# Strassen's algorithm for 18 of the 22 up-projection pairs of the second FFN

## The reference

```
x = x + 0.5 * rmsnorm(swiglu(rmsnorm(x, g0), w1, w3, w2), g1)      # first FFN
x = x + rmsnorm(mixer(rmsnorm(x, g2)), g3)                          # mLSTM, S5, short convolution
x = x + 0.5 * rmsnorm(swiglu(rmsnorm(x, g4), w1', w3', w2'), g5)    # second FFN
swiglu(x, w1, w3, w2) = (silu(x @ w1) * (x @ w3)) @ w2
```

## Time and profile before

| | us |
|---|---|
| median of 3 runs | 1088.48 (1088.02 to 1089.86) |
| span of the profiled execution | 1087.4 |
| TensorE busy | 1077.2 (99%) |
| VectorE busy | 533.9 (49%) |
| ScalarE busy | 358.4 (33%) |
| GpSimd busy | 95.5 (9%) |
| chain that ended last: TensorE's share | 95% |

### The profile page before, as it was taken

One profiled execution on the slowest core, in us unless ns is written; L12 is line 12 of the kernel. 1 busy time (PEld: TensorE's weight loads), 2 busy tenths in 40 slices (PEclk: granted clock), 3 DMA queues, 4 the chain that ended last, 5 costly groups with the idle time before them and its releaser, 6 DMA issues.

```text
span 1087.4 us, 21585 instructions
## 1 busy us (share of the span) xinstructions
PE 1077.2 (99%) x8945; PEld 1063.8 (98%) x8945; DVE 533.9 (49%) x929; ACT 358.4 (33%) x527; POOL 95.5 (9%) x169
## 2 busy tenths in 40 slices
PE   8999999999999999999999999999999999999998
PEld 8999999999999999998999999999999999999997
DVE  6444524343333369685656787743323343324346
ACT  5322114222122345321537543532212222122232
POOL 0000725920000000340000000000000000000000
PEclk9999999999999999999999999999999999999999
DMA  7223232222222241123421134132222222222232
GB/s 253 83 78 96 80 94 81 93 83 91 82 88 82 78 136 40 60 78 122 135 62 59 60 117 148 40 98 95 80 94 80 94 83 91 85 90 89 76 88 83
DMA packets 30338, 99.13 MB, mean 91 GB/s; under 512 B 3652, under 2 KB 6084, under 8 KB 30152
## 3 DMA queue, kind: packets, MB, share of 16 engines
q1 hardware_dynamic: 30280, 98.33, 28.7%
HBM read 93.58 MB, written 4.74 MB: 90 GB/s over the span
## 4 chain that ended last, share of the span: by engine, by line
PE 95%; DVE 2%; ACT 1%; issue 1%; DMA 0%; SPq 0%; DVEq 0%; ACTq 0%
PE ps L2013 77%; PE ps L2038 6%; PE ps L2107 3%; PE ps L2481 2%; PE ps L2125 1%; PE ps L2045 1%; PE ps L2050 1%; PE ps L2305 0%; PE ps L2264 0%; DMA x<-xT 0%; PE ps L2255 0%; PE ps L2331 0%; DVE wl L1019 0%; PE ps L2298 0%; PE ps L2272 0%
## 5 line engine op out<-in xcount | busy, mean ns | idle before, releaser
L1019 DVE TENSOR_TENSOR wl<-raw,wh 128x1024 fp32r<-128x1024 f32 (+1 forms) x145 | 178.1, 1229 | 409.2 <-ACT wh L563 408.6
L2013 PE MATMUL ps<-xh,wh 128*128 128x272 f32 x1616 | 336.3, 289 | 1.2 <-DVE k L1437 1.0
L2013 PE MATMUL ps<-xl,wh 128*128 128x272 f32 x1616 | 333.7, 288 | 0.0
L2013 PE MATMUL ps<-xh,wl 128*128 128x272 f32 x1616 | 332.8, 287 | 0.0
L563 ACT CAST wh<-raw 128x1024 fp32r<-128x1024 f32 (+1 forms) x145 | 150.6, 1038 | 422.4 <-PE ps L2013 419.6
L2013 PEld LDWEIGHTS ps<-xh,wh 128*128 128x128 f32 x1616 | 253.0, 188 | 2.5 <-issue 1.4
L2013 PEld LDWEIGHTS ps<-xl,wh 128*128 128x128 f32 x1616 | 254.1, 189 | 0.0
L2013 PEld LDWEIGHTS ps<-xh,wl 128*128 128x128 f32 x1616 | 252.9, 188 | 0.0
L2013 PE MATMUL ps<-hh,wh 128*128 128x272 f32 x608 | 126.3, 289 | 0.5 <-DVE hl L1040 0.5
L2013 PE MATMUL ps<-hl,wh 128*128 128x272 f32 x608 | 125.4, 287 | 0.0
L2013 PE MATMUL ps<-hh,wl 128*128 128x272 f32 x608 | 125.3, 287 | 0.0
(11 more groups left out here) (483 smaller groups left out, 1181.9 us busy)
## 6 DMA issues: line engine op xcount, KB each, us to landing
raw<-w SPq DMA_DIRECT2D x118, 512.0 KB, 3.5
raw<-win SPq DMA_DIRECT2D x25, 512.0 KB, 3.5
raw<-w SPq DMA_DIRECT2D x16, 384.0 KB, 3.1
raw<-wout SPq DMA_DIRECT2D x8, 512.0 KB, 3.6
o_yT<-x SPq DMA_DIRECT2D x8, 272.0 KB, 2.2
cs<-cT SPq DMA_DIRECT2D x4, 516.0 KB, 4.4
o_sC<-cs SPq DMA_DIRECT2D x4, 516.0 KB, 6.4
x<-xT SPq DMA_DIRECT2D x3, 544.0 KB, 6.8
```

The lines of the kernel that those rows point to most:

```text
L1019: V.tensor_tensor(wl[par][:, 0:cols], raw[par][:, 0:cols], wh[par][:, 0:cols].bitcast(F32), ALU.subtract).then_inc(split_done, 1)
L2013: last = mm(ps[:, bank + s, 0:HALF], w[:, kk * P:(kk + 1) * P], a[:, kk, s * HALF:(s + 1) * HALF], start=(kk == 0 and i == 0), stop=(kk == ...
```

## The change

Only the second FFN is changed. Its parts become PARTS2 = 4, 6, 6, 6. Part 0 stays as it was (8 up units), but its hidden tiles get the token factor on both sides (scaled, gated). The 18 pairs behind it are multiplied otherwise: the two 1024-row weight tiles of a pair (w3 and w1) form a 2 x 2 block matrix with blocks of 4 tiles (KHP = 512 columns of SBUF), the input, normed and split in its two column halves and two row halves, another. Winograd's form of Strassen's algorithm makes the 2 x 2 block product from seven block products (p1 to p7) of 4 tiles x 3 matmuls of 272 columns, and sums of blocks before and behind.

- The **input's sums** (four forms; base_x are the plain blocks) are made once, in part 0: VectorE writes the normed input xn (normed, 8 times), GpSimd makes the form sums, ScalarE rounds them (hi_form), VectorE takes low parts (lo_form). The three base blocks are rounded into the room of xh and xl when unit u0+7 is done.
- The **weights' sums** for each pair: S1 and S3 on VectorE (sum_13, 1024 columns), S2 and S4 on GpSimd (512 columns each). They lie in raw's place; the pairs are loaded, 1 MB each, into two buffers `pairs`. Each block or sum is rounded by ScalarE (hi_...) and its low part taken by VectorE (lo_...).
- The **sums behind** are made partly by accumulation in PSUM, partly by ScalarE copies (keep_p1, keep_p5, keep_u2) and VectorE adds that write into PSUM (c11, c12, c22).
- The up and down loops of this FFN are written out and not rolled.

TensorE's waits: p1 for hidden(j-2); p2 for lo_g(j) and silu(j-2); p3 for lo_4(j) and keep_p5(j); p4 for lo_a22(j) and c22(j); p5 for lo_12(j); p6 for keep_p1(j); p7 for lo_3(j) and keep_u2(j). The diff follows, cut to its core and ordered by engine (the names of the new buffers, the semaphores and helpers of like form are left out). SP:

```diff
+PARTS2 = (4, 6, 6, 6)
...
+            def load_pair(j):
+                if j == 0:
+                    spe.wait_ge(out_dma, 16 * EARLY_STORES)
+                elif j == 1:
+                    spe.wait_ge(form_lo, 1)
+                else:
+                    spe.wait_ge(a22_lo, j - 1)
+                    spe.wait_ge(s4_sum, j - 1)
...
+            def ffn2():
+                for u in range(4, 2 * PARTS2[0]):
+                    load(FFN2_BASE + u, (FFN2_BASE + u) % 2, A["w13_1"][u])
+                load_pair(0)
+                load_pair(1)
```

ScalarE (the other hi_ and keep_ steps have the form of these):

```diff
+            def hi_g(j):
+                pair_full(j)
+                if j % N6:
+                    act.wait_ge(p1_done, j)
+                else:
+                    act.wait_ge(unit_used, down_unit(j // N6, KD - 2) + 3)
+                nc.scalar.copy(wh[1][:], pairs[j % 2][:, 2 * KHP:4 * KHP]).then_inc(g_hi, 1)
+            def hi_12(j):
+                act.wait_ge(s2_sum, j + 1)
+                if j % N6:
+                    act.wait_ge(p6_done, j)
...
+                silu(hb + 2, 0)
+                hi_form(0, form_hi_t[:, 2], form_t3[:], 1.0)
+                hi_form(1, form_hi_t[:, 0], xn[:, 0, 1], 1.0)
+                hi_form(2, form_hi_t[:, 1], form_t24[:], -1.0)
+                hi_form(3, form_hi_t[:, 3], form_t24[:], 1.0)
+                up_split(u0 + 7)
+                hidden_hi(hb + 2, 0, 2)
...
+                        for i, src in enumerate((xn[:, 0, 0], xn[:, 1, 0], xn[:, 1, 1])):
+                            nc.scalar.copy(base_hi_t[:, i], src).then_inc(form_hi, 1)
+                        act.wait_ge(form_lo, 4)
...
+                            hi_4(j)
+                            hi_a22(j)
+                            if j > j0:
+                                silu_pair(j - 1)
+                            keep_p1(j)
+                            if last:
+                                act.wait_ge(p1_done, j + 1)
+                                down(0)
+                            else:
+                                hi_g(j + 1)
+                            keep_p5(j)
+                            keep_u2(j)
...
+                                hi_3(j + 1)
+                                hi_12(j + 1)
+                            if j > j0:
+                                hidden_hi(FT4 + j - 1, 0, j - 1 - j0)
```

VectorE, part 0 and one pair:

```diff
+                up_first(hb, 0, u0)
+                scaled(hb, 0)
+                gated(hb, 0, u0 + 1)
+                up_first(hb + 1, 1, u0 + 2)
+                hidden_lo(hb, 0, 0)
+                scaled(hb + 1, 1)
+                up_lo(u0 + 5)
+                gated(hb + 1, 1, u0 + 3)
+                hidden_lo(hb + 1, 1, 1)
+                for kk in range(KD):
+                    normed(kk)
+                up_lo(u0 + 6)
+                up_first(hb + 2, 0, u0 + 4)
+                lo_form(0, form_lo_t[2][:], form_t3[:], form_hi_t[:, 2], 1.0)
+                lo_form(1, form_lo_t[0][:], xn[:, 0, 1], form_hi_t[:, 0], 1.0)
+                lo_form(2, form_lo_t[1][:], form_t24[:], form_hi_t[:, 1], -1.0)
+                scaled(hb + 2, 0)
+                lo_form(3, form_lo_t[3][:], form_t24[:], form_hi_t[:, 3], 1.0)
+                up_lo(u0 + 7)
+                gated(hb + 2, 0, u0 + 5)
...
+                            if not last:
+                                sum_13(j + 1)
+                            if j > j0:
+                                c12(j - 1)
+                            lo_4(j)
+                            lo_a22(j)
+                            c11(j)
+                            if last:
+                                down(0)
+                            else:
+                                lo_g(j + 1)
+                            if j > j0:
+                                c22(j - 1)
...
+                                lo_3(j + 1)
+                                lo_12(j + 1)
+                            if j > j0:
+                                hidden(j - 1)
+                                hidden_lo(FT4 + j - 1, 0, j - 1 - j0)
```

GpSimd:

```diff
+            pool.wait_ge(xn_ready, KD)
+            pool.wait_ge(out_dma, 16 * EARLY_STORES)
+            G.tensor_tensor(form_t3[:], xn[:, 1, 1], xn[:, 0, 1], ALU.subtract).then_inc(form_raw, 1)
+            pool.wait_ge(form_raw, 1)
+            G.tensor_tensor(xn[:, 0, 1], xn[:, 0, 0], xn[:, 0, 1], ALU.subtract).then_inc(form_raw, 1)
+            pool.wait_ge(form_raw, 2)
+            G.tensor_tensor(form_t24[:], xn[:, 0, 1], xn[:, 1, 1], ALU.add).then_inc(form_raw, 1)
+            pool.wait_ge(form_lo, 3)
+            G.tensor_tensor(form_t24[:], form_t24[:], xn[:, 1, 0], ALU.subtract).then_inc(form_raw, 1)
+            for j in range(NG):
+                w = pairs[j % 2]
+                pool.wait_ge(s13_sum, j + 1)
+                if j:
+                    pool.wait_ge(s4_sum, j)
+                G.tensor_tensor(sums[:, S2B], sums[:, S1B], w[:, A11B], ALU.add).then_inc(s2_sum, 1)
+                if j:
+                    pool.wait_ge(s4_lo, j)
+                pool.wait_ge(s2_sum, j + 1)
+                G.tensor_tensor(sums[:, S4B], sums[:, S2B], w[:, A12B], ALU.add).then_inc(s4_sum, 1)
```

TensorE, one pair and the end of a part:

```diff
+                            p2(j)
+                            p1(j)
+                            if j > j0:
+                                p7(j - 1)
+                            p5(j)
+                            p6(j)
+                            if j > j0:
+                                p4(j - 1)
+                            p3(j)
+                        p7(j)
+                        enter_down(0)
+                        down(0, range(0, 3))
+                        p4(j)
+                        down(0, range(3, n - 1))
+                        enter_down(1)
+                        down(1, range(0, n - 1))
+                        down(0, range(n - 1, n))
+                        down(1, range(n - 1, n))
```

More of the change, by code:

```diff
@@ L35 @@
 PARTS = (8, 8, 6)
[L36 removed]
+PARTS2 = (4, 6, 6, 6)
+assert sum(PARTS) == FT and sum(PARTS2) == FT and PARTS2[-1] == PARTS[-1]
+NG = sum(PARTS2[1:])
+KH = KD // 2
+KHP = KH * P
+FORM = KH * HALF
 UNIT = KD * P
@@ L1108, in ffn, with sum_13 @@
                     yb += KD
+            def sum_13(j):
+                dve.wait_ge(pair_in[j % 2], 32 * (j // 2 + 1))
+                if j % N6:
+                    dve.wait_ge(s12_lo, j)
+                    dve.wait_ge(s3_lo, j)
+                else:
+                    dve.wait_ge(split_done, down_unit(j // N6, KD - 1) + 3)
+                w = pairs[j % 2]
+                V.tensor_tensor(two(sums[:, 2 * KHP:]), two(w[:, KHP:3 * KHP]),
+                                w[:, A21B].unsqueeze(1).to_broadcast([P, 2, KHP]), ALU.add).then_inc(s13_sum, 1)
@@ new lines, in low, with lo_g, lo_12, lo_3 @@
+            def low(hi, j, dst, src, rounded, done):
+                dve.wait_ge(hi, j + 1)
+                V.tensor_tensor(dst, src, rounded.bitcast(F32), ALU.subtract).then_inc(done, 1)
+            def lo_g(j):
+                low(g_hi, j, wl[1][:], pairs[j % 2][:, 2 * KHP:4 * KHP], wh[1][:], g_lo)
+            def lo_12(j):
+                low(s12_hi, j, two(wl[0][:]), sums_12(), two(wh[0][:]), s12_lo)
+            def lo_3(j):
+                low(s3_hi, j, s3_w[j % 2][1][:], sums[:, S3B], s3_w[j % 2][0][:], s3_lo)
@@ new lines, in lo_a22, with lo_4, c11, c12 @@
+            def lo_a22(j):
+                low(a22_hi, j, a22_w[j % 2][1][:], pairs[j % 2][:, A22B], a22_w[j % 2][0][:], a22_lo)
+            def lo_4(j):
+                low(s4_hi, j, s4_w[1][:], sums[:, S4B], s4_w[0][:], s4_lo)
+            def c11(j):
+                dve.wait_ge(p1_kept, j + 1)
+                b = ps[:, set_of(j), 0:HALF]
+                V.tensor_tensor(b, b, p1_keep, ALU.add).then_inc(c11_done, 1)
+            def c12(j):
+                dve.wait_ge(p3_done, j + 1)
+                dve.wait_ge(u2_kept, j + 1)
+                c = ps[:, bank_c(j), 0:HALF]
+                V.tensor_tensor(c, c, u2_keep, ALU.add).then_inc(c12_done, 1)
@@ new lines, in c22, with hidden @@
+            def c22(j):
+                dve.wait_ge(p7_done, j + 1)
+                dve.wait_ge(p5_kept, j + 1)
+                a, d = bank_a(j), set_of(j) + 3
+                V.tensor_tensor(ps[:, d, 0:HALF], ps[:, a, 0:HALF], p5_keep(j), ALU.add).then_inc(c22_done, 1)
+            def hidden(j):
+                dve.wait_ge(p4_done, j + 1)
+                dve.wait_ge(silu_ready, FT4 + j + 1)
+                dve.wait_ge(c22_done, j + 1)
+                dve.wait_ge(h_lo, FT4 + j)
+                V.scalar_tensor_tensor(halves(dve_t[:, 0]), c2_of(j), -1.0, halves(act_t[:, 0]), ALU.mult, ALU.mult)\
+                    .then_inc(h_ready, 1)
@@ new lines, in hidden_lo, with scaled, gated @@
+            def hidden_lo(hm, s, mi):
+                dve.wait_ge(h_hi, hm + 1)
+                V.tensor_tensor(hl[:, mi, :], dve_t[:, s], hh[:, mi, :].bitcast(F32), ALU.subtract).then_inc(h_lo, 1)
+            def scaled(hm, s):
```

(15 more changed lines are left out.)

321 lines of the change are left out of this document (310 added, 11 removed).

## The result

The changed kernel takes **1101.74 us** (median of 4 runs, 1100.35 to 1104.63), the kernel before beside it 1089.06. The ratio is 1.0117, 95% interval 1.0101 to 1.0134: 12.7 us slower, where 6.4 was forecast. The profiled execution took 1100.35 us, its span is 1098.5 us, 11.1 more than the earlier trace rows.

What follows compares the result with a forecast made beforehand. The second FFN was taken as bound by TensorE's number of matmuls unless operands come late. -27.0 + 15.0 + 1.5 + 1.3 + 0.9 + 14.7 = +6.4 gave 1094.9 us, range 1079 to 1103 (own range 1090 to 1100).

Steps and rivals of the forecast that it cites:

- The saving: TensorE in the 18 pairs: seven products for eight, 216 matmuls fewer at 0.125 us, -27.0 us.
- u0+7: Last up unit of part 0: its weights come late behind the form sums, start 733.0 for 718.05, +15.0 us.
- The turns: VectorE and GpSimd operations with two SBUF inputs exclude each other and run in order of request, in head and pair loop.
- Half rate: After TensorE's 13 us idle before u0+7, matmuls run 3 us at the 1.2 GHz level: +1.5 us (0 to 3.4).
- The rest of part 0: Down units after u0+7: low parts late behind base-block roundings and low parts, +1.3 us (0.5 to 2.5).
- the first pair: At the first pair, weight sums and low parts take turns after short down units: +0.9 us (0 to 1.8).
- The pair loop: Turns with GpSimd's S2 and S4 delay p4 and each part's second p2: 4.9 us a part, +14.7 for three.
- pair loads 2 us: In the pair loop, the loads of the weight pairs were given 2 us of slack, so no wait.
- rival 2: Pair loop longer: PSUM writes at 0.9 us, or keeps and waits dearer by 1 us together; +8, 1103 us; chance 0.18.
- rival 1: Pair loop: same blocking, but GpSimd's S4 slips behind lo_g, p4 at 11.0 not 12.04; 1083.7 us; chance 0.22.
- rival 3: No blocking between these VectorE and GpSimd operations: u0+7 at 729.9, loop 10.75 us; 1077.9 us; chance 0.13.
- The step that failed: At each part's end p7, three tiles of down unit 0 and down unit 1 cover the last hidden: no added wait.

Runs made afterwards that it cites:

- the last kernel: Changed kernel with GpSimd's sums on VectorE, part 0's evacuations on ScalarE, head reordered, down unit 1 early, p3 before p4: 1063.70 us, ratio 0.9757 to the kernel before.
- The first experiment: Changed kernel with one order edit at each part's end: two tiles of down unit 1, unit 0's last, then unit 1's rest: 1096.23 us.

## Why the prediction was right or wrong

The direction was right and the size was not: 12.7 us for 6.4, by the spans 11.1.

- **The saving** of 27.0 us was right, 26.6 where nothing is late. 239 matmuls in the middle of the last kernel's pair loop (760 to 790) follow 0.1256 us apart, 799 of the kernel before (900 to 1000) 0.1253: the price of 0.125 held.
- **u0+7** was forecast at 733.0 and started at 731.75; u0+6 at 714.2 and started at 714.21. The turns in the head came nearly as worked out, with two of four forms stretched to 3.4 us. "Advanced Engine Details and Errata" of the Trainium skill (VectorE Performance Modes) names blocking only between GpSimd and VectorE's two-port modes, and has no such mode for tensor_tensor; the 1.66 and 1.96 us, and their going in the kernels where GpSimd is small or silent, show that it blocks all the same.
- **Half rate** was 1.7 for 1.5 and lies where it was put. It shows in u0+6 too (715.1 to 718.6), where the wait for u0+7 hides it. Its price elsewhere was left out: a wait of 2.1 to 2.4 us was followed by some 3.5 us at half rate, which cost 1.5, in some executions and by none in others. The profiled changed kernel had none of those; its median, 1.4 us above the profile, may hold some; that is not shown.
- **The rest of part 0** and the first pair, 1.7 and 1.6 for 1.3 and 0.9, were in their ends. Of the 1.5 us at 747.48, about 0.7 are again the evacuation queued behind the low part, for which the prediction had no term.
- **The pair loop** cost 11.7 for 14.7. The mechanism of the turns is as said (lo_4 behind S2, lo_g behind S4, c22 behind both). At p4 a part was to have waits of 0.5, 1.1, 0.5 and 1.1 (with the 1.8 at p2 that is 5.0; the sum took 4.9). There are two, of 1.5 and 1.2, 2.8 a part. The size of the first is luck: the turns give 0.46 of it, the forecast's 0.5, and the third pair's load gives 1.0 to 1.2, where the prediction had "pair loads 2 us" of slack. The third and fourth waits did not come. p2's wait is 1.1 on the mean for 1.8. Writes into PSUM cost 0.44, as taken, so rival 2's ground fell; S4 did not slip behind lo_g (rival 1), and the blocking is there (rival 3).
- **The step that failed** is one clause: "At a part's end p7, three tiles of down unit 0 and down unit 1 cover the last hidden; the tail from there is as before". I asked only whether the hidden tile was covered. The weights of the third down unit were not followed: they need the buffer of down unit 0, which this order holds until 0.8 us before the end of unit 1; and its sums need unit 0's PSUM banks, which VectorE evacuates only behind the third unit's low part. That costs 2.06 us, three times. The span missed the forecast by 4.7 us; this step alone is 6.2, and the loop's 3.0 go the other way. Before, unit 0 ended a whole unit earlier. The first experiment takes it away alone, with no other work touched.
- **A second slack that failed** is that of the pair loads: 3.3 us at p4, inside the loop's 11.7. No experiment moved the loads alone; the case rests on the constant distances above.

Of the signs that I named, idle near 720 to 733, stretched low parts, p4 and the second p2 late all came. Waits at p6 came only when an order of mine made them. One not named came too: the wait of sum_13 for the third pair's load.

## What to carry to other kernels

Before a second engine is given part of an engine's work, ask whether the two can run at once: here 512 columns on VectorE cost 0.69 us, on GpSimd 1.29, and a VectorE operation beside it lost 0.75 to 2.3 us; the offloaded work was dearer even for the engine that it should relieve. When units on a ring of two buffers are interleaved, follow the buffers and not only the data: whichever unit is finished first frees the next load and the next banks, and two that finish together leave the third bare. When a profile names what ended a wait, compare the distance from its end with that of a plain case: here 0.74 for 0.06 us gave away a second condition. And a saving on the bounding engine came through only where the others' queues were ordered by when their result is wanted: the same algorithm gave 12.7 us of loss or 25.5 of gain by queue order and engine alone.
